# A fused two-block network on one core: the recurrence's gate products in the format of the other products, each as three

## The reference, cut to what matters

```python
xr = causal_dwconv(xr, conv_rnn_w[l], conv_rnn_b[l])        # 4 taps along the sequence
xb = x.reshape(B, S, N_RNN_BLOCKS, RNN_BLOCK)               # 8 blocks of 128 channels
r = jax.nn.sigmoid(jnp.einsum('bsnc,ncd->bsnd', xb, w_rg).reshape(B, S, D_RNN) + b_rg)
i = jax.nn.sigmoid(jnp.einsum('bsnc,ncd->bsnd', xb, w_ig).reshape(B, S, D_RNN) + b_ig)
log_a = -LRU_C * r.astype(jnp.float32) * jax.nn.softplus(-lam.astype(jnp.float32))
a = jnp.exp(log_a)
mult = jnp.sqrt(-jnp.expm1(2.0 * log_a))
u = x.astype(jnp.float32) * i.astype(jnp.float32) * mult
# h = a * h_before + u along the sequence; the result is h * gelu(yr)
```

## Time and profile before

| | us |
|---|---|
| median of 3 runs | 1737.51 (1737.26 to 1738.64) |
| the profiled execution | 1740.86 |
| its span, first to last instruction | 1739.1 |
| TensorE matmul busy | 1705.9 (98%) |
| GpSimd busy | 1454.7 (84%) |
| VectorE busy | 1056.5 (61%) |
| ScalarE busy | 544.1 (31%) |

### The profile page before, as it was taken

The page is one execution under the profiler, slowest core; times in us unless marked ns, Lnnn a source line. Parts: engine busy times, 40 slices in busy tenths (PEclk is TensorE's granted clock), DMA queues, the critical chain, the costliest instruction groups (busy, mean ns, idle before and its releaser), DMA issues.

```text
span 1739.1 us, 33168 instructions
## 1 busy us (share of the span) xinstructions
PE 1705.9 (98%) x11518; PEld 1488.8 (86%) x11518; DVE 1056.5 (61%) x1596; ACT 544.1 (31%) x825; POOL 1454.7 (84%) x2245
## 2 busy tenths in 40 slices
PE   8899999999999999999999999999999999999998
PEld 5677776678898888888899999999999999999887
DVE  6688998845696545422677766866685455555102
ACT  5235664321323322100443444444443211111001
POOL 4567896568999988999689888988897999999885
PEclk9999999999999999999999999999999999999999
DMA  9942332233323333333222222222222332333332
GB/s 346 388 146 80 94 91 97 97 98 88 95 83 98 107 97 96 97 106 100 73 86 86 75 83 76 86 85 74 86 86 73 97 96 87 94 96 97 97 109 97
DMA packets 55387, 184.57 MB, mean 106 GB/s; under 512 B 6721, under 2 KB 9953, under 8 KB 55298
## 3 DMA queue, kind: packets, MB, share of 16 engines
q1 hardware_dynamic: 52066, 177.53, 32.3%
q10 hardware_dynamic: 3232, 5.77, 0.9%
HBM read 178.56 MB, written 4.72 MB: 105 GB/s over the span
## 4 chain that ended last, share of the span: by engine, by line
PE 79%; POOL 8%; DVE 5%; issue 3%; DMA 2%; ACT 1%; DVEq 1%; SPq 1%; ACTq 0%; POOLq 0%
PE gp L448 25%; PE gp L449 24%; PE gp L450 24%; POOL Wlo L431 5%; POOL Whi L428 2%; POOL probe L427 1%; DMA raw<-units 1%; DMA AW<-ada 1%; PE A L591 1%; PE A L819 1%; PE A L870 1%; PE A L624 0%; PE A L872 0%; PE A L862 0%; DVE AW L1441 0%
## 5 line engine op out<-in xcount | busy, mean ns | idle before, releaser
L431 POOL TENSOR_TENSOR Wlo<-raw,Whi 128x256 fp32r<-128x256 f32 x1120 | 964.3, 881 | 46.7
L448 PE MATMUL gp<-XNhi,Whi 128*128 128x258 f32 (+3 forms) x2320 | 737.1, 318 | 12.2 <-DVE XNlo L1450 4.5
L449 PE MATMUL gp<-XNlo,Whi 128*128 128x258 f32 (+3 forms) x2320 | 725.8, 313 | 0.0
L450 PE MATMUL gp<-XNhi,Wlo 128*128 128x258 f32 (+3 forms) x2320 | 724.2, 312 | 0.0
L448 PEld LDWEIGHTS gp<-XNhi,Whi 128*128 128x128 f32 x2320 | 437.3, 188 | 51.5 <-issue 14.4
L449 PEld LDWEIGHTS gp<-XNlo,Whi 128*128 128x128 f32 x2320 | 437.4, 189 | 28.6 <-issue 2.4
L450 PEld LDWEIGHTS gp<-XNhi,Wlo 128*128 128x128 f32 x2320 | 436.8, 188 | 26.8
L427 POOL TENSOR_TENSOR probe<-raw 1x1 f32<-1x1 f32 x560 | 176.0, 314 | 218.8 <-PE gp L450 154.1
L428 POOL TENSOR_SCALAR Whi<-raw 128x512 fp32r<-128x512 f32 x560 | 343.3, 613 | 0.0
L448 PE MATMUL gp<-AChi,Whi 128*128 128x512 f32 (+1 forms) x518 | 197.2, 381 | 0.4 <-POOL Wlo L431 0.4
L449 PE MATMUL gp<-AClo,Whi 128*128 128x512 f32 (+1 forms) x518 | 196.9, 380 | 0.0
(11 more groups left out here) (348 smaller groups left out, 2257.3 us busy)
## 6 DMA issues: line engine op xcount, KB each, us to landing
raw<-units SPq DMA_DIRECT2D x280, 512.0 KB, 3.6
AW<-ada SPq DMA_DIRECT2D x40, 512.0 KB, 8.6
AWL<-ada SPq DMA_DIRECT2D x8, 512.0 KB, 3.7
bias_rows<-RB ACTq DMA_DIRECT2D x1, 2560.0 KB, 21.2
H<-xT SPq DMA_DIRECT2D x4, 512.0 KB, 6.0
BIAS<-bias_rows ACTq DMA_DIRECT2D x1, 2048.0 KB, 7.9
out<-H SPq DMA_DIRECT2D x8, 256.0 KB, 2.2
WG<-gatew ACTq DMA_DIRECT2D x8, 128.0 KB, 2.0
```

The costliest lines, as they stand in the source:

```text
L431: ins = pool.tensor_tensor(lo[:, c:c + UNIT // 4], src[:, c:c + UNIT // 4], hi[:, c:c + UNIT // 4].bitcast(F32), ALU.subtract)
L448: pe.matmul(dst, Whi[s][:, k, :], rhi, start=start, stop=False)
L449: pe.matmul(dst, Whi[s][:, k, :], rlo, start=False, stop=False)
L450: return pe.matmul(dst, Wlo[s][:, k, :], rhi, start=False, stop=stop)
```

## The change

The gates' weights and inputs are rounded into new tiles `WGhi` and `XChi` by ScalarE, their rests `WGlo` and `XClo` are made by VectorE, and each gate product becomes three. On ScalarE the copies stand between `recurrence(b-1)` and block b's gelu; on VectorE the rests stand behind the second round of top-k (for block 0, behind its taps). TensorE waits for the rests in place of the taps and the weights.

```diff
+                XChi, XClo = [sb(n, [P, S], F32R, fx) for n in ("XChi", "XClo")]
...
+                    WGhi, WGlo = [sb(n, [P, 2 * P], F32R, fr) for n in ("WGhi", "WGlo")]
...
-                pe.wait_ge(gate_in, b * 16 + 16)
-                pe.wait_ge(xc_ready, b + 2)
+                pe.wait_ge(gx_ready, b + 1)
                 pe.wait_ge(ig_ready, b * 2 + 1)
                 for r in range(2):
-                    pe.matmul(A45[:, r * 512:(r + 1) * 512], WG[:, r * P:(r + 1) * P], XC[b % 2][:, :],
-                              start=True, stop=True).then_inc(gate_mm, 1)
+                    o, whi, wlo = A45[:, r * 512:(r + 1) * 512], WGhi[:, r * P:(r + 1) * P], WGlo[:, r * P:(r + 1) * P]
+                    pe.matmul(o, whi, XChi[:, :], start=True, stop=False)
+                    pe.matmul(o, whi, XClo[:, :], start=False, stop=False)
+                    pe.matmul(o, wlo, XChi[:, :], start=False, stop=True).then_inc(gate_mm, 1)
...
                 if b:
                     recurrence(b - 1)
+                act.wait_ge(gate_in, b * 16 + 16)
+                act.activation(WGhi[:, :], WG[:, :], ACT.Copy)
+                act.wait_ge(xc_ready, b + 2)
+                act.activation(XChi[:, :], XC[b % 2][:, :], ACT.Copy)
+                act.drain().then_inc(gx_high, 1)
                 ps, free = psum(b * 3 + 1)
                 act.wait_ge(rnn_done, max(b, 1))
...
+            def gate_rests(b):
+                if b == KC:
+                    return
+                dve.wait_ge(gx_high, b + 1)
+                dve.tensor_tensor(WGlo[:, :], WG[:, :], WGhi[:, :].bitcast(F32), ALU.subtract)
+                dve.tensor_tensor(XClo[:, :], XC[b % 2][:, :], XChi[:, :].bitcast(F32), ALU.subtract)
+                dve.drain().then_inc(gx_ready, 1)
+
             for b in range(KC + 1):
...
                     ins.then_inc(xc_ready, 1)
+                if b == 0:
+                    gate_rests(0)
                 if b:
                     xc, gy = XC[(b - 1) % 2], GY[(b - 1) % 2]
                     take((1, 2, 3))
...
                     take((1, 2, 3))
+                    gate_rests(b)
                     if b == KC:
```

More of the change, by code:

```diff
@@ L299, in build @@
         mult_ready, u1_done, rnn_done = sem("mult_ready"), sem("u1_done"), sem("rnn_done")
-        rgate_ready = sem("rgate_ready")
+        rgate_ready, gx_high, gx_ready = sem("rgate_ready"), sem("gx_high"), sem("gx_ready")
         sg_ready, merge_done = sem("sg_ready"), sem("merge_done")
```

## The result

The changed kernel takes **1753.93 us** (median of 4 runs, 1753.08 to 1757.06); the kernel before, run beside it, 1737.45 (4 runs). The ratio is 1.0092 [1.0080, 1.0105]: slower by 16.5 us at the medians. A second series of five runs gave 1753.78 (1752.47 to 1756.76) against 1738.89, ratio 1.0087 [1.0073, 1.0101], 14.9 us.

A forecast was written before the change was run, and what follows sets the result against it. Two equal chains, TensorE's products and eviction through gelu to the bank, set a block's 18.21 us. Block 0 10.1 us later, seven periods of 19.16 us, bumps +0.5, last gates -0.35: +13.8 us, 1751.3 us, range 1744 to 1757.

The forecast's parts named there:

- 0.5 for bumps: Over the recurrence's blocks: an allowance of +0.5 us for irregular delays like those seen in the kernel before.
- 0.35 given back: At the last gates: shorter TensorE gate products save 0.35 us, since ScalarE's sigmoid waits for both gates.
- two chains of equal length: Running block: TensorE's products, and eviction, taps, top-k, root, gelu, bank, both set the 18.21 us; neither has slack.
- (a) Gates, 1.37 us: TensorE's gate products per block: six at 0.228 us replace 1.72 us, 0.35 less, counting only where TensorE's chain is longer.
- (b) Copies, +0.95 us a block: ScalarE's two copies between root and gelu lengthen the second chain by 0.95 us, making the period 19.16 us.
- (c) "1.6 us: covered, by 0.36 us": VectorE's rests behind the second top-k round add 1.6 us; 18.8 us of work stays under the 19.16 us period.
- VectorE or GpSimd becomes the bound, 19.7 a block: Rival for running blocks: VectorE work and GpSimd splits slow each other, 19.7 us a block, 1755.1 us in all; 8%.
- (d) Block 0, +10.1 us: First block: ScalarE waits for the taps before gelu, TensorE stalls at unit 3, the first T comes 10.1 us later.
- Clock falls at each 1.3 us of idle time: Rival for running blocks: TensorE's clock drops at each bank wait, seven more times 1.7 us, 1763 us; 4%.
- The sum: Whole kernel: block 0's delay, seven periods of 19.16 us, bumps and the last gates' give-back total +13.8 us.
- The conversion from the profiled execution to the medians: Whole kernel: the profiled execution stands 3.35 us above the median 1737.51, so 1754.7 in its terms becomes 1751.3.

## Why the prediction was right, and where it wasn't

The forecast was 1751.3 us in a range of 1744 to 1757, slower with 0.94. Both medians, 1753.93 and 1753.78, lie in it, and the mechanism was the one named. In the profile's terms it had T0 to T8 at +13.7 and 0.5 for bumps, and 0.35 given back, +13.8; the trace has +15.3 and nothing given back. Three terms were mis-sized, and two of the errors cancel in part.

- **What bounds a block** (two chains of equal length): right. Moving gelu out of the way alone gives 0.12 us a block, and what delays gelu counts in full.
- **(a) Gates, 1.37 us:** six starts 0.235 us apart, 1.41 us, and TensorE's own chain is 17.76 us long against 18.09 (the periods in which it ran freely, with gelu ahead of the root, in either kernel). Right, and it buys nothing in a running block, as said; that it also moves GpSimd's splits 0.3 us forward against T was not thought of. The 0.35 us at the last gates don't show: T8 to the end is 0.07 longer, and executions scatter by more.
- **(b) Copies, +0.95 us a block:** 0.95 in the changed kernel, 0.92 by the run with the copies alone; 6.6 us over seven periods. The row L1302, 417 ns, stood for 0.40, and L1176 for 0.62. What the Trainium skill's "ScalarE: Activation LUTs", section "What ACT_TABLE_LOAD costs", gives for such activations, 186 ns + 0.833 ns per element, is 0.399 and 0.613 us, and the trace agrees; its 2.66 us for a change of table don't fit here, where gelu again starts 1.30 us behind the start of its load.
- **(c) "1.6 us: covered, by 0.36 us": this step failed**, in its size and in its conclusion. The rests measured 2.0 us with their drain (0.74 and 1.22 us in the changed kernel). The row L1338 (481 ns) that I took for the 256-wide one was no measure for it. 17.2 + 2.0 = 19.2 is as long as the 19.16 that was to cover it, so nothing was left of the 0.36 us, as the run with the rests alone shows: 19.0 to 19.2 with no copy on the chain. In the changed kernel the cost came by another way, though. VectorE still has 0.7 us to spare at the taps; the rests set VectorE and GpSimd in another place to each other, and the root's argument came 0.54 us later, some 3 us over the six blocks from block 2 on. The rival "VectorE or GpSimd becomes the bound, 19.7 a block" had the right figure, 19.7, and half of the reason.
- **(d) Block 0, +10.1 us:** +8.5 by the trace. The order of events was right, gelu at 129.65, 18.8 us behind T0 (forecast: 134.3 - 113.35 = 20.9), and so was the clock: unit 3 took 7.72 us from 130.39 to 138.11 for 24 products that take 5.47 at 0.228, a loss of 2.25 against 1.7. What failed is that the taps would end when they did before. They ended at T0+16.69 instead of T0+18.82, 2.1 us earlier, of which the clock took 0.5 back. Before, GpSimd worked beside VectorE; here it stood still, as TensorE did, for which it works at most two units ahead (POOL 0.00 in 124 to 135).
- **Clock falls at each 1.3 us of idle time** (4%): no. TensorE idles 1.6 us in every block, and the clock is 1.00 in 190 to 230 us. The swinging clock that the Trainium skill, "TensorE: Matmul & The Clock Gate", section "A second HAM failure mode: psum-queue depth-cycling", tells of for small idle spells, and that the prediction weighed, does not show in this pattern.
- **The sum:** 13.8 - 1.5 (block 0) + 2.65 (periods, beyond the 0.5 allowed for bumps) + 0.4 (not given back) = 15.3. By medians it is 16.5 and 14.9. The total is this near partly by luck: block 0 was put too high and the blocks too low.

The conversion from the profiled execution to the medians was sound as well: that execution had been a late one, by 3.35 us, and its T0 lay 2.5 us behind that of the changed kernel's first profile, which was at its own median.

## What to carry to other kernels

Where a chain from engine to engine has no slack, ask of each new instruction what it stands ahead of in its own engine's order: two copies put between a root and a gelu cost their full 0.95 us in each block on an engine that was a third idle, and 0.56 us a block came back when they moved into a wait. "Covered by 0.36 us" is no cover when the work's duration comes from a row of another kind; take both ends of it against the cover and give that rival its weight. And a wait added for the steady state also stands in the first block, where what it waits for may be eleven microseconds away.

## What the runs showed of the hardware

**VectorE's operations on two tiles have durations that depend on what GpSimd does at that moment.** The clearest are in block 0, where GpSimd is at work before the change and idle after it. VectorE in the kernel before, eight small operations and the taps:

```profile
126.27 2.78 DVE L1589 SCALAR_TENSOR_TENSOR MSQ<-H,V,MRS 128x16 f32<-128x16 f32 x8
129.12 3.05 DVE L1597 SCALAR_TENSOR_TENSOR rnn_xc<-XR,V,rnn_xc 128x512 f32<-128x512 f32 x3
```

and in the changed kernel:

```profile
123.83 1.24 DVE L1597 SCALAR_TENSOR_TENSOR MSQ<-H,V,MRS 128x16 f32<-128x16 f32 x8
125.15 2.40 DVE L1614 SCALAR_TENSOR_TENSOR rnn_xc<-XR,V,rnn_xc 128x512 f32<-128x512 f32 x3
```

GpSimd was busy 4.87 of the 5.90 us from 126.27 in the first case. In the second it was busy 0.09 us from 123.8 to 125.1, and not at all behind that. From first start to last end it is 5.9 us against 3.7, which is the 2.1 us by which block 0's taps ended earlier than forecast. The run with the wait alone has the same 1.24 and 2.40 us. A 128x512 operation on two tiles is at 0.69 us undisturbed and at 1.02 to 1.28 with a Wlo pair begun ahead of it, and the pair itself goes from 1.44 to 1.88 or 2.33. Such a pair, or any row with x2, holds two instructions, and how they meet is seen only with each by itself. In the rows of single instructions above, whichever comes second ends 0.54 to 0.61 us behind the end of the other, whenever it began. In the changed kernel the first Wlo (224.29 to 225.03) takes its undisturbed 0.74 us. rnn_u starts in it, at 224.55, and ends at 225.57, 0.54 us behind it. The second Wlo starts in rnn_u, at 224.98, and ends at 226.17, 0.60 us behind that. In the block of 18.98 us rnn_u is first, keeps its 0.69 us and ends at 224.43, and the first Wlo ends at 225.03, the root's argument at 225.58 and the second Wlo at 226.19. The Trainium skill, "SBUF — State Buffer", section "SBUF: two separate sides", says that of a VectorE instruction with two SBUF inputs and a GpSimd instruction that reads SBUF the one that starts first has the shared port pair for its whole length, and that the other is blocked so long. The trace agrees: what is left to do behind the other's end is nearly a whole undisturbed operation, so at most 0.15 us of the second one's work can have been done before.

**Such a meeting repeats itself.** The place of GpSimd in a block follows TensorE's (the pair at T+7.76 to T+7.87 in blocks 2 to 7 of the changed kernel), and TensorE's the period, so a kernel falls into a pattern of one block (19.7 each time) or two (18.98 and 19.68, 18.75 and 19.52) and keeps it.

**The clock comes back late after a long idle time, and a regular short one leaves it alone.** The 8.86 us of idle time at block 0 were followed by 4.5 us at 0.51, as the 3.05 us of the kernel before were by 3.5 us at 0.51; the 1.6 us in each later block were followed by none.
